# One layer of a streaming encoder on one core: the first two column pairs as 16 block products with four operands each, their kept units made in the second macro tile, and the output weights' sums kept in DRAM

## The chip, the core and the metric

The kernel runs on one core of a Trainium2 chip. The metric is the device time of one execution in microseconds (us), lower is better. Engines are named as the profile names them: PE is the matrix engine (TensorE), PEld its weight loads, DVE the vector engine (VectorE), ACT the scalar engine (ScalarE), POOL is GpSimd, and SP is the engine whose queue issues most DMAs here.

## The reference, cut to what matters

`x` is 4096 tokens by 1024 channels, `mem` 256 rows by 1024, all float32. One layer is computed:

```python
h = rms_norm(x, pre_norm)
proj = h @ w_in                    # 1024 x 5120: b, c, u of 1024 each, gate of 1536, mq of 512
p, gate, mq = proj[..., :3072], proj[..., 3072:4608], proj[..., 4608:]
z = c_gate * u; mix = b_gate * (conv_w[0]*z[t-2] + conv_w[1]*z[t-1] + conv_w[2]*z[t])
mem_o = memory_cross_attention(mq, mem, mem_norm, w_mem_kv)     # 4 heads of 128, 256 keys
y = (concat([mix, mem_o]) * silu(gate)) @ w_out                 # 1536 x 1024
x = x + rms_norm(y, post_norm)
```

## The kernel before, in words

**Products in three passes.** Each float32 operand is split into a high part (ACT copies it to `fp32r`, which rounds it) and a low part (DVE subtracts the high part). A block product of 512 x 128 weights with 512 x 512 tokens is 4 slices of the contraction by 3 matmuls (high x high, high x low, low x high), so 12 matmuls of 512 columns (`product`, lines L1438 to L1440).

**Seven products for eight.** The input projection is done by macro tiles of 1024 tokens (`MACROS` = 4) and by pairs of 2 x 128 output columns (`PAIRS` = 20). A pair over a macro tile is a 2 x 2 by 2 x 2 block product (halves of the contraction, of the columns and of the tokens), made with 7 products R1, R5, R6, R3, R7, R2, R4 instead of 8 (Strassen and Winograd's scheme). For this it needs sums of blocks on both sides. `x_in` holds the four normed blocks Y11, Y21 (tile 0) and Y12, Y22 (tile 1); `token_sum` (L1027) makes four sums of them in place, 128 x 2048 each; `operand_hi` (L737) and `operand_lo` (L1031) split the seven results into `hop_hi` and `hop_lo`. On the weights' side `weight_sum` (L1055) makes four sums for each pair out of the four raw chunks X11, X21, X22, X12, and `build_hi` (L692) and `split_lo` (L1060) put seven *units* for each pair into four `slots`.

**Units are made once.** Macro tile 0 builds its 140 units and SP writes each to `w_split` in DRAM (L502); macro tiles 1 to 3 load them back (`load_unit`, L485). `KINDS` gives what a pair is: two `m` (gate of the memory branch, through SiLU), then four groups of `c`, `u`, `b`, `g` (the convolution's inputs and its gate), then two `q`. Macro tiles 0 to 2 run them in this order; the last runs `q`, `q` first, since its steps also carry the memory attention.

**The start.** Tokens' squares are summed (ACT L664, DVE L1258 and L1260), a column sum on PE (`sum_first`, L1444) gives the mean squares, ACT the root, DVE the inverse and four diagonal blocks (`inverse`), PE spreads them over the partitions (`spread`, L1459), and DVE scales the rows (`norm`, L1002). The first two pairs run side by side (`FIRST_TWO`: product r of pair 0, then of pair 1, for r in turn), in separate banks. Pair 2 follows, its first product being product 14 counted from 0.

**The output projection** (stage `OUT`, 16 pairs of token tiles) uses the same scheme for the convolution's 1024 rows of `w_out`: the four blocks of `w_conv` are loaded into `x_in` in the last pair's time, `token_sum` makes the same four sums, and the seven splits follow. Each OUT pair has two more products, M0 and M1 (`add_memory`), for the memory branch; they use `WM_HI` and `WM_LO`, which lie in `x_in`'s place (as `x_r`, split at L963, L967 and L1414), so they can be made only when the sums are done with.

**What sets the order.** All queues are written by hand. Each engine runs its list in order, and a wait on a semaphore holds all that stands behind it. PE does product `step` of the macro tile, ACT and DVE follow it step by step with the evacuations (`evacuate`, `add`, `use`) and with the unit four steps ahead (`ahead`). In the last pair before a macro tile, ACT and DVE also make its operands. PE's `multiply` waits for its unit, for the operand (only in a macro tile's first pair), and for its bank to be read.

Of the kernel before, what the change touches and what calls it, by code (L numbers as in the profile page):

```python
# [5 lines left out]
P = 128  # L6
D = 1024
SEQ = 4096
T = 512
NT = SEQ // T  # L10
SUB = T // P
KT = D // P
# [22 lines left out]
UNITS0 = PAIRS * PRODUCTS  # L35
# [3 lines left out]
LAST_ROWS = list(range(18, PAIRS)) + list(range(18))  # L39
R1, R5, R6, R3, R7, R2, R4, M0, M1 = range(PRODUCTS + 2)  # L40
# [17 lines left out]
OUT_X_AT = {122: 0, 123: 1, 124: 3, 125: 2}  # L58
# [12 lines left out]

FIRST_TWO = [(p, r) for r in range(PRODUCTS) for p in range(2)]
ORDER = FIRST_TWO + [(p, r) for p in range(2, ALL_PAIRS) for r in range(PRODUCTS)]

# [13 lines left out]
BUILT = {u: n for n, u in enumerate(sorted([u for (p, r), u in UNIT_OF.items() if p < PAIRS or p >= ALL_PAIRS]  # L88
# [6 lines left out]


X11, X21, X22, X12, G0, G1 = range(6)
PLACE, TIMES, WAS = {}, {}, {}
for _p in list(range(PAIRS)) + list(range(ALL_PAIRS, ALL_PAIRS + OUT_PAIRS)):
    for _x in (X11, X21, X22, X12) if _p < PAIRS else (X11, X21, X22, X12, G0, G1):  # L100
        if _p < 2:
            _n = 3 * _p + _x if _x != X12 else CHUNKS + _p
        elif _p < PAIRS:
            _n = (0, 1, 3, 4, 2, 5)[(4 * _p + _x - 8) % CHUNKS]
# [10 lines left out]
def row_of(p):  # L115

    return p % PAIRS if p < (MACROS - 1) * PAIRS else LAST_ROWS[p % PAIRS]

# [10 lines left out]
def built_pair(p):  # L129

    return p if p < PAIRS else PAIRS + p - ALL_PAIRS


def trunk(nc, x, x_t, mem, in_gains, post_g, conv, w_in, w_kv, w_conv, w_mem, out):
# [6 lines left out]
    with ExitStack() as ctx:  # L141
# [14 lines left out]
        first_x12 = at("first_x12", R4 * HK * T * 4, [2, HALF])  # L156
# [40 lines left out]
        raw_kv = [raws[:, 0:2, :], raws[:, 2:4, :]]  # L197
        v_t = at("v_t", Q_AT + 4 * KB, [NM])
# [24 lines left out]
        bank_x = [psum[:, 2, :], psum[:, 6, :]]  # L223
        bank_b = [psum[:, 3, :], psum[:, 7, :]]
# [10 lines left out]
        w_split = nc.dram_tensor("w_split", [UNITS0, P, UNIT], f32, kind="Internal").ap()  # L235
        mem_kept = nc.dram_tensor("mem_kept", [NT * SUB, P, MH, P], f32, kind="Internal").ap()
        q_kept = nc.dram_tensor("q_kept", [MACROS, MH, 2, P, T], f32, kind="Internal").ap()
        m_kept = nc.dram_tensor("m_kept", [MACROS, MH, 2, P, T], f32, kind="Internal").ap()
        g_kept = nc.dram_tensor("g_kept", [NT * SUB, 2, P, HK, P], f32, kind="Internal").ap()
# [13 lines left out]

        w_sum = sem("w_sum")
        w_hi = sem("w_hi")
        w_lo = sem("w_lo")
        unit_done = sem("unit_done")

# [76 lines left out]

        WM_HI = [x_r[:, 0, 0:HK, :], x_r[:, 1, 0:HK, :]]
# [13 lines left out]
        def raw(p, x):  # L350
            n = PLACE[p, x]
            return raws[:, n, :] if n < CHUNKS else first_x12[:, n - CHUNKS, :]
# [4 lines left out]
        def raw_used(eng, p, x):  # L357

            if x in (X11, X21):
# [19 lines left out]
        def unit_source(p, r):  # L379
# [3 lines left out]
            return sums_in(p)[:, 0 if r in (R5, R3) else 1, :]  # L383

        def sums_in(p):

            return sqt if p == 1 else st_w
# [3 lines left out]
        SECOND = {R3: zb[:, 1, HALO:], R7: zb[:, 3, HALO:], R2: zb[:, 0, HALO:], R4: zb[:, 2, HALO:]}  # L391

        def temp(p, r):
            return SECOND[r] if p == 1 else TEMP[r]

        def silu_count(p, r):

            if p < 2:
                return 2 * ORDER_OF[r] - 1 + p
# [6 lines left out]
        def temp_free(eng, p, r):  # L406

            kind = kind_of(p)
            if kind in "qcy":
                eng.wait_ge({R3: c12_done, R7: c22_done, R2: c11_done}[r], p + 1)  # L410
# [5 lines left out]
        def sums_before(p, r):  # L416

            if p < 2:
                return 2 * min(r, 4) - 1 + p
# [29 lines left out]
        def normed_for(m, block):  # L449

            return 2 * KT * m + (("11", "12", "22", "21") if m == 0 else ("11", "21", "12", "22")).index(block) * HK + HK
# [6 lines left out]
        def _(sp):  # L458
            def load_raw(p, x):
# [3 lines left out]
                if p < PAIRS:  # L463
                    src = w_in[p, x]
# [11 lines left out]
            def load_x(n, m):  # L476
                tile, half = n % 2, n // 2
                src = x_t[2 * m + tile] if m < MACROS else w_conv[tile]
# [1197 lines left out]
```

## Time and profile before

| | us |
|---|---|
| median of 3 runs | 2240.54 (2238.6 to 2240.66) |
| the profiled execution, its time | 2240.83 |
| its span, first to last instruction | 2238.7 |
| PE busy | 2181.0 (97%) |
| DVE busy | 1213.8 (54%) |
| ACT busy | 734.6 (33%) |
| DMA | 462.64 MB, 207 GB/s on the mean |

PE is busy for 97% of the span, so what can be won beside fewer matmuls lies where PE isn't busy or is at its lower clock. A matmul's record is longer (0.39 us) than the distance between two starts (0.23 us), since they are pipelined: distances between starts tell the rate, and a distance of 0.43 us is the lower of PE's two clocks. The chain of waits that ended last is 88% PE.

### The profile page before, as it was taken

The page shows a single profiled execution, that of the slowest core. Times are in us where ns is not written, and L with a number is a line of the kernel's source. Part 1 is how long each engine was busy: PE and PEld are TensorE (multiplying, and loading weights), DVE is VectorE, ACT ScalarE, POOL GpSimd, SP SyncE. Part 2 cuts the span into 40 slices and gives each one's busy share as a digit, 9 for nine tenths or more (in the row PEclk, how much of TensorE's full clock was granted, in tenths as well). Part 3 has the DMA queues.
Part 4 walks back from the last instruction along what each step waited for, and adds up shares of the span by engine and source line. Part 5 has one row for each costly group of instructions (what it writes and reads, how often), then busy time and mean ns, then how long its engine had stood idle before and what let it go on. Part 6 is the DMA issues. An engine that isn't in the chain of part 4 may idle for free.

```text
span 2238.7 us, 26842 instructions
## 1 busy us (share of the span) xinstructions
PE 2181.0 (97%) x9950; PEld 1805.9 (81%) x9950; DVE 1213.8 (54%) x1917; ACT 734.6 (33%) x1328; POOL 100.8 (5%) x155
## 2 busy tenths in 40 slices
PE   5999999999999999999999999999999899999998
PEld 3788888788888888888888888888888688888886
DVE  7677787614443351444335337576755755555554
ACT  4433433411121131212113333535442533333332
POOL 0000000000000000000000000000010000000000
PEclk9999999999999999999999999999999999999999
DMA  4886676677566577756667666666667433434331
GB/s 170 309 307 255 256 272 245 253 262 256 187 209 212 194 245 268 252 186 211 207 213 259 226 215 197 215 201 215 198 203 295 129 130 109 132 132 132 127 119 65
DMA packets 140880, 462.64 MB, mean 207 GB/s; under 512 B 15664, under 2 KB 15696, under 8 KB 137808
## 3 DMA queue, kind: packets, MB, share of 16 engines
q1 hardware_dynamic: 119952, 385.40, 49.6%
q0 software_dynamic: 20800, 75.53, 10.4%
q8 instruction: 81, 1.33, 0.2%
q14 instruction: 47, 0.39, 0.1%
HBM read 328.75 MB, written 132.12 MB: 206 GB/s over the span
## 4 chain that ended last, share of the span: by engine, by line
PE 88%; DVE 6%; issue 2%; ACT 2%; DMA 1%; SPq 0%; DVEq 0%; ACTq 0%
PE banks L1438 29%; PE banks L1440 29%; PE banks L1439 29%; DVE hop_lo L1031 2%; PE banks L1553 1%; DVE x_in L1027 1%; DMA slots<-w_split 1%; ACT probs L811 0%; ACT hop_hi L737 0%; PE banks L1444 0%; DVE slots L1060 0%; PE banks L1459 0%; DMA raws<-in_w_kv 0%; DVE x_in L1002 0%; DVE rmax L1181 0%
## 5 line engine op out<-in xcount | busy, mean ns | idle before, releaser
L1438 PE MATMUL banks<-hop_hi,slots 128*128 128x512 f32 x2688 | 1055.9, 393 | 18.7 <-DVE slots L1060 6.7
L1439 PE MATMUL banks<-hop_lo,slots 128*128 128x512 f32 x2688 | 1048.8, 390 | 0.0
L1440 PE MATMUL banks<-hop_hi,slots 128*128 128x512 f32 x2688 | 1048.3, 390 | 0.0
L1438 PEld LDWEIGHTS banks<-hop_hi,slots 128*128 128x128 f32 x2688 | 506.1, 188 | 131.1 <-DVE slots L1060 14.4
L1440 PEld LDWEIGHTS banks<-hop_hi,slots 128*128 128x128 f32 x2688 | 506.0, 188 | 106.4
L1439 PEld LDWEIGHTS banks<-hop_lo,slots 128*128 128x128 f32 x2688 | 506.5, 188 | 103.7 <-issue 1.4
L1060 DVE TENSOR_TENSOR slots<-raws,slots 128x512 fp32r<-128x512 f32 x154 | 105.3, 690 | 130.9 <-ACT slots L692 130.4
L748 ACT ACTIVATE s<-banks 128x512 f32<-128x512 f32 x95 | 56.9, 599 | 343.8 <-PE banks L1440 343.0
L1112 DVE TENSOR_TENSOR u<-banks,u 128x512 f32<-128x512 f32 x55 | 38.0, 690 | 235.7 <-PE banks L1440 235.7
L692 ACT ACTIVATE slots<-raws 128x512 fp32r<-128x512 f32 x154 | 95.5, 626 | 150.4 <-PE banks L1440 126.3
L692 ACT ACTIVATE slots<-st_w 128x512 fp32r<-128x512 f32 x140 | 87.9, 628 | 158.8 <-PE banks L1440 121.2
L1060 DVE TENSOR_TENSOR slots<-st_w,slots 128x512 fp32r<-128x512 f32 x140 | 96.1, 686 | 29.4 <-ACT slots L692 29.0
L756 ACT ACTIVATE u<-banks 128x512 f32<-128x512 f32 x95 | 56.7, 597 | 156.2 <-PE banks L1440 156.2
L752 ACT ACTIVATE p<-banks 128x512 f32<-128x512 f32 x95 | 56.8, 597 | 149.6 <-PE banks L1440 149.6
L1438 PE MATMUL banks<-x_r,slots 128*128 128x512 f32 x256 | 100.3, 392 | 3.5 <-DVE x_r L1414 3.5
L1439 PE MATMUL banks<-x_r,slots 128*128 128x512 f32 x256 | 100.3, 392 | 0.0
L1440 PE MATMUL banks<-x_r,slots 128*128 128x512 f32 x256 | 100.1, 391 | 0.0
L1031 DVE TENSOR_TENSOR hop_lo<-x_in,hop_hi 128x2048 fp32r<-128x2048 f32 x35 | 79.6, 2286 | 27.1 <-ACT hop_hi L737 27.1
L737 ACT ACTIVATE hop_hi<-x_in 128x2048 fp32r<-128x2048 f32 x35 | 66.1, 1909 | 51.7 <-DVE x_in L1027 37.6
L620 POOL DMA_DIRECT2D g_kept<-mix x32 | 28.3, 888 | 985.5 <-DVE mix L1137 985.5
L811 ACT ACTIVATE probs<-banks,nmax 128x256 f32<-128x256 f32 x128 | 58.9, 473 | 29.9 <-DVE nmax L1183 29.9
L1196 DVE TENSOR_TENSOR pt_lo<-banks,pt_hi 128x512 fp32r<-128x512 f32 x64 | 41.2, 686 | 47.7 <-ACT pt_hi L819 47.2
(163 smaller groups left out, 1938.0 us busy)
## 6 DMA issues: line engine op xcount, KB each, us to landing
slots<-w_split SPq DMA_DIRECT2D x420, 512.0 KB, 3.4
w_split<-slots SPq DMA_DIRECT2D x140, 512.0 KB, 3.2
raws<-in_w_in SPq DMA_DIRECT2D x78, 256.0 KB, 3.9
x_in<-in_x_t SPq DMA_DIRECT2D x16, 1024.0 KB, 6.9
g_kept<-mix POOLq DMA_DIRECT2D x32, 512.0 KB, 6.6
raws<-g_kept SPq DMA_DIRECT2D x64, 256.0 KB, 3.9
x_zb<-in_x POOLq DMA_DIRECT2D x22, 512.0 KB, 4.2
out_x<-x_zb POOLq DMA_DIRECT2D x21, 512.0 KB, 4.1
```

Of the source, the lines that this page charges most:

```text
L692: nc.scalar.activation(slots[:, slot, 0, :], src, ACT.Copy).then_inc(w_hi, 1)
L737: nc.scalar.activation(hop_hi[:, r, :, :], Y_OF[r], ACT.Copy).then_inc(hop_hi_done, 1)
L748: nc.scalar.activation(temp(p, R2), a, ACT.Copy).then_inc(s1_done, 1)
L752: nc.scalar.activation(temp(p, R7), bank_x[p == 1], ACT.Copy).then_inc(p5_done, 1)
L756: nc.scalar.activation(temp(p, R3), a, ACT.Copy).then_inc(u2_done, 1)
L811: nc.scalar.activation(probs[:, n % 2, s, :], scores[:, s, :], ACT.Exp, scale=SCALE, bias=nmax[:, s:s + 1], accum_out=rsum[:, s:s + 1]).th ...
L1031: nc.vector.tensor_tensor(hop_lo[:, r, :, :], Y_OF[r], hop_hi[:, r, :, :].bitcast(f32), ALU.subtract).then_inc(hop_lo_done, 1)
L1060: nc.vector.tensor_tensor(slots[:, slot, 1, :], src, slots[:, slot, 0, :].bitcast(f32), ALU.subtract).then_inc(w_lo, 1)
L1196: nc.vector.tensor_tensor(pt_lo[:, a, :], probs_t[:, a, :], pt_hi[:, a, :].bitcast(f32), ALU.subtract).then_inc(pt_lo_done, 1)
L1438: nc.tensor.matmul(dst, a, c, start=first, stop=False, skip_group_check=True)
L1439: nc.tensor.matmul(dst, a, d, start=False, stop=False, skip_group_check=True)
L1440: return nc.tensor.matmul(dst, b, c, start=False, stop=last, skip_group_check=True)
```

## The change

1. **The first two pairs (both `m`) of macro tile 0** are no longer made with 7 products each. They are 16 plain block products (`multiply_first`), on four blocks of tokens and four raw weight chunks for each pair, without any sum. The eight chunks are split where `hop_hi` and `hop_lo` later have operands R7 and R4. The list runs tile 0 first (both halves of the contraction, both pairs), then tile 1; each of its four quarters needs one more block of tokens.
2. **The start is put in another order:** Y11 is split in two halves of its own, tile 0 is normed whole before tile 1's sums are used, and PE runs 50 matmuls of 128 x 128 float32 on constants (`warm`) ahead of the first column sums and 16 more ahead of the first product.
3. **Their 14 units** (rows 0 and 1 of `w_split`) are built in macro tile 1 instead, where the two `m` pairs stand behind the 16 convolution pairs (`SECOND_ROWS`, `LATE`): ACT and DVE build them four steps ahead, SP keeps them, and their raw chunks are loaded again. Everything that counts pairs from the first is counted from pair 2 (`seven_to`).
4. **The sums of `w_conv`'s blocks** are made in macro tile 2, a quarter at a time (4 x 4 sums of 128 x 512 on DVE, `out_sum`), and kept in DRAM (`sums_kept`). The seven operands of OUT are then loaded: four in the steps 122 to 125 as before, three more when the operand that held the place has been split. No `token_sum` is left in the OUT stage, and the splits follow each other one step apart.

Lines with only "..." stand for what is left out.

```diff
+DIRECT = 2
+UNITS0 = (PAIRS - DIRECT) * PRODUCTS
+SECOND_ROWS = list(range(DIRECT, 18)) + list(range(DIRECT)) + list(range(18, PAIRS))
+LATE = [PAIRS + SECOND_ROWS.index(n) for n in range(DIRECT)]
+LATE_RAW_AT = 96
+WARM = (50, 16)
-OUT_X_AT = {122: 0, 123: 1, 124: 3, 125: 2}
+OUT_X_AT = {122: R1, 123: R5, 124: R6, 125: R3}
+SUMS_MACRO = MACROS - 2
+SUMS_LOAD_AT = [1 + 10 * k for k in range(HK)]
+SUMS_AT = [a + 3 for a in SUMS_LOAD_AT]
+SUMS_KEEP_AT = [a + 8 for a in SUMS_LOAD_AT]
+FIRST_UNITS = [(p, x) for x in (X11, X21, X12, X22) for p in range(DIRECT)]
+FIRST = FIRST_UNITS + [(p, x) for half in ((X11, X21), (X12, X22)) for p in range(DIRECT) for x in half]
...
 SP: first loads
             load_x(0, 0)
             load_x(2, 0)
-            load_raw(0, X11)
+            for p in range(DIRECT):
+                load_raw(p, X11)
             load_x(1, 0)
+            for p in range(DIRECT):
+                load_raw(p, X21)
             load_x(3, 0)
...
 SP: macro tiles 1 to 3
+                        if p in LATE:
+                            keep_unit(p, r)
+                        else:
+                            load_unit(p, r)
+                        if m == SUMS_MACRO:
+                            out_sums_ahead(now)
...
+                        if now == (PAIRS - 1) * PRODUCTS + R5:
+                            sp.wait_ge(hop_lo_done, OUT * PRODUCTS + R1 + 1)
+                            load_out(R7)
+                        if now == (PAIRS - 1) * PRODUCTS + R6:
+                            sp.wait_ge(hop_lo_done, OUT * PRODUCTS + R5 + 1)
+                            load_out(R2)
...
+            sp.wait_ge(hop_lo_done, OUT * PRODUCTS + R6 + 1)
+            load_out(R4)
...
 ACT and DVE: units ahead
-                if m == 0 and n < UNITS0:
-                    build(*ORDER[n])
+                if m < 2 and n < STEPS and (m == 0 or PAIRS + n // PRODUCTS in LATE):
+                    build(m * PAIRS + n // PRODUCTS, n % PRODUCTS)
...
 ACT: in the last pair, then after it
-                    if i == PAIRS - 1 and r != R6 and (m + 1 < OUT or r != R4):
+                    if i == PAIRS - 1 and m + 1 < OUT and r != R6:
                         operand_hi(m + 1, {R1: R1, R5: R5, R3: R6, R7: R3, R2: R7, R4: R2}[r])
+                    if i == PAIRS - 1 and m + 1 == OUT and r != R4:
+                        operand_hi(OUT, r)
                 if n == 0:
-                    operand_hi(OUT, R2)
+                    operand_hi(OUT, R4)
...
 DVE: the start
             for n in range(1, HK + 1):
                 add_first(0, n)
+            first_units_lo(X11)
             inverse(0)
             add_first(1, 1)
             for k in range(HK):
                 norm(0, k)
+            for half in range(2):
+                two = slice(2 * half, 2 * half + 2)
+                dve.wait_ge(first_hop_hi, half + 1)
+                nc.vector.tensor_tensor(hop_lo[:, R1, two, :], Y11[:, two, :], ...)
+            add_first(1, 2)
+            first_units_lo(X21)
+            for n in range(3, HK + 1):
                 add_first(1, n)
+            for k in range(HK, KT):
+                norm(0, k)
+            first_units_lo(X12)
             inverse(1)
+            operand_lo(0, R2)
+            first_units_lo(X22)
+            for k in range(KT):
+                norm(1, k)
+            ... hop_lo[:, R6, :, :] from Y12, then operand_lo(0, R3)
             token_sum(0, 0)
+            build(DIRECT, R1)
+            operand_lo(0, R5)
...
 DVE: in the last pair before OUT
+                    if i == PAIRS - 1 and m + 1 == OUT and r != R1:
+                        operand_lo(OUT, r - 1)
...
 PE: the start
+            def multiply_first(n):
+                p, x = FIRST[n]
+                half = int(x in (X12, X22))
+                bank = first_output((n // 8 * 4) + (n % 4))[3]
+                if n < len(FIRST_UNITS):
+                    pe.wait_ge(first_unit_lo, n + 1)
+                if n and n % 4 == 0:
+                    pe.wait_ge(hop_lo_done, n // 4)
+                ... 12 matmuls
+            def warm(n):
+                for _ in range(n):
+                    nc.tensor.matmul(psum[:, 7, 0:P], ones[:], ones[:], start=True, stop=True)
             pe.wait_ge(consts_set, 5)
+            warm(WARM[0])
             sum_first(0)
             spread(0)
+            warm(WARM[1])
+            multiply_first(0)
+            multiply_first(1)
             sum_first(1)
+            multiply_first(2)
+            multiply_first(3)
             spread(1)
-            for p, r in FIRST_TWO:
-                multiply(p, r)
+            for n in range(4, len(FIRST)):
+                multiply_first(n)
```

## Rows read from the trace of the kernel before

**Rows 1.** Page: span, part 1 (busy time, share, instructions)
```profile
span 2238.7 us, 26842 instructions
PE 2181.0 (97%) x9950; PEld 1805.9 (81%) x9950; DVE 1213.8 (54%) x1917; ACT 734.6 (33%) x1328; POOL 100.8 (5%) x155
```
**Rows 2.** PE by stretch: stretch and length, busy (instructions), granted clock, DMA share, GB/s
```profile
100.00:385.00 285.00, 285.00 (x1263) 1.00 0.74 270
```
**Rows 3.** PE in order of time, start: start us, us, what [idle before <-releaser]
```profile
12.95 1.84 PE L1444 MATMUL banks<-ones,first_sq 128*128 128x1 f32 x8 [12.95 <-DVE first_sq L1260]
16.26 2.07 PE L1459 MATMUL banks<-acc,ones 128*128 128x512 f32 x2 [1.48 <-DVE acc L996]
29.97 0.76 PE L1438 MATMUL banks<-hop_hi,slots 128*128 128x512 f32 x1 [0.22 <-DVE hop_lo L1031]
...
41.53 0.79 PE L1438 MATMUL banks<-hop_hi,slots 128*128 128x512 f32 x1 [4.23 <-DVE slots L1060]
...
46.39 0.63 PE L1440 MATMUL banks<-hop_hi,slots 128*128 128x512 f32 x1
...
82.77 0.47 PE L1438 MATMUL banks<-hop_hi,slots 128*128 128x512 f32 x1 [2.38 <-ACT mix L782]
...
85.61 0.39 PE L1438 MATMUL banks<-hop_hi,slots 128*128 128x512 f32 x1
...
88.33 0.39 PE L1438 MATMUL banks<-hop_hi,slots 128*128 128x512 f32 x1
```
**Rows 4.** DVE in order of time, start
```profile
16.12 1.22 DVE L1258 TENSOR_TENSOR first_sq<-first_sq 128x1024 f32<-128x1024 f32 x1
18.37 2.72 DVE L1002 SCALAR_TENSOR_TENSOR x_in<-x_in,gains,banks 128x512 f32<-128x512 f32 x4 [1.03 <-PE banks L1459]
...
27.54 2.28 DVE L1031 TENSOR_TENSOR hop_lo<-x_in,hop_hi 128x2048 fp32r<-128x2048 f32 x1
```
**Rows 5.** ACT in order of time, start
```profile
3.48 0.20 ACT L862 ACTIVATE ysd<-eps 128x1 f32<-128x1 f32 x1 [1.45 <-POOL ident L599]
...
11.59 2.00 ACT L664 ACTIVATE first_sq<-x_in 128x1024 f32<-128x1024 f32 x2 [1.15 <-DMA x_in<-in_x_t]
...
16.88 1.14 ACT L692 ACTIVATE slots<-raws 128x512 fp32r<-128x512 f32 x2
21.13 1.91 ACT L737 ACTIVATE hop_hi<-x_in 128x2048 fp32r<-128x2048 f32 x1 [3.11 <-DVE x_in L1002]
```
**Rows 6.** PE in order of time, small matmuls at the full clock
```profile
186.26 0.95 PE L1444 MATMUL banks<-ones,acc 128*128 128x1 f32 x8
187.07 0.48 PE L1438 MATMUL banks<-hop_hi,slots 128*128 128x512 f32 x1
```
**Rows 7.** PE in order of time, around one head's transposes
```profile
1339.14 1.03 PE L1553 MATMUL banks<-ident,probs 128*128 128x128 f32 x8
1339.93 0.47 PE L1438 MATMUL banks<-hop_hi,slots 128*128 128x512 f32 x1
```
**Rows 8.** PE in order of time, where the OUT stage begins
```profile
1736.76 0.47 PE L1438 MATMUL banks<-hop_hi,slots 128*128 128x512 f32 x1 [1.75 <-DVE p L1112]
...
1746.88 0.47 PE L1438 MATMUL banks<-hop_hi,slots 128*128 128x512 f32 x1 [1.68 <-ACT s L748]
...
1760.87 0.47 PE L1438 MATMUL banks<-hop_hi,slots 128*128 128x512 f32 x1 [2.01 <-DVE mix L1112]
...
1767.30 0.64 PE L1438 MATMUL banks<-x_r,slots 128*128 128x512 f32 x1 [3.45 <-DVE x_r L1414]
```
**Rows 9.** DMA issues: what, times, KB each, median us to landing
```profile
slots<-w_split SPq DMA_DIRECT2D x420, 512.0 KB, 3.4
w_split<-slots SPq DMA_DIRECT2D x140, 512.0 KB, 3.2
x_in<-in_w_conv SPq DMA_DIRECT2D x4, 1024.0 KB, 7.3
```
**Rows 10.** PE in order of time, after the wait that ends macro tile 0
```profile
428.71 0.47 PE L1438 MATMUL banks<-hop_hi,slots 128*128 128x512 f32 x1 [2.04 <-DVE zb L1112]
...
430.80 0.63 PE L1438 MATMUL banks<-hop_hi,slots 128*128 128x512 f32 x1
```

More of the change, by code:

```diff
@@ L334, in trunk @@
         Y_OF = [Y11, Y12, Y12, Y22, Y11, Y21, Y21]
+        OUT_OF = [Y11, Y12, Y21, Y22, Y11, Y12, Y21]
+        OUT_LOAD = [(0, 1), (1, 1), (2, 1), (3, 1), (0, 2), (1, 2), (2, 2)]
         WM_HI = [x_r[:, 0, 0:HK, :], x_r[:, 1, 0:HK, :]]
@@ L491, in _ @@
             load_x(3, 0)
[L492 to L506 removed]
+            for x in (X12, X22):
+                for p in range(DIRECT):
+                    load_raw(p, x)
@@ L507, in _ @@
+            for x in (X11, X21, X22, X12):
+                load_raw(DIRECT, x)
+            for p, r in ORDER[:UNITS0]:
+                keep_unit(p, r)
+                if r == R1 and p < PAIRS - 1:
                     load_raw(p + 1, X11)
                     load_raw(p + 1, X21)
-                if r == R3 and 1 < p < PAIRS - 1:
+                if r == R3 and p < PAIRS - 1:
                     load_raw(p + 1, X22)
@@ L1279, in _ @@
                 norm(0, k)
-            for n in range(2, HK + 1):
+            for half in range(2):
+                two = slice(2 * half, 2 * half + 2)
+                dve.wait_ge(first_hop_hi, half + 1)
+                nc.vector.tensor_tensor(hop_lo[:, R1, two, :], Y11[:, two, :], hop_hi[:, R1, two, :].bitcast(f32),
+                                        ALU.subtract).then_inc(first_hop_lo, 1)
+            add_first(1, 2)
+            first_units_lo(X21)
+            for n in range(3, HK + 1):
@@ L1319, in _ @@
-            build(*ORDER[len(FIRST_TWO) + 3])
-            for p in range(2, ALL_PAIRS):
+            build(DIRECT, R6)
+            build(DIRECT, R3)
+            token_sum(0, 3)
+            operand_lo(0, R7)
+            operand_lo(0, R4)
+            for p in range(DIRECT, ALL_PAIRS):
                 m, i = divmod(p, PAIRS)
@@ L1347, in _ @@
                     ahead(m, step)
-                    if i == PAIRS - 1:
+                    if m == SUMS_MACRO:
+                        for k, first in enumerate(SUMS_AT):
+                            if first <= step < first + 4:
+                                out_sum(k, step - first)
+                    if i == PAIRS - 1 and m + 1 == OUT and r != R1:
+                        operand_lo(OUT, r - 1)
+                    if i == PAIRS - 1 and m + 1 < OUT:
                         if r in (R5, R6, R7, R2, R4):
@@ L1368, in _ @@
                             token_sum(m + 1, 0)
-                    elif step == 130:
-                        token_sum(OUT, 0)
                     if m + 1 == MACROS:
```

427 lines of the change are left out of this document (223 added, 204 removed).

## The prediction

> **What bounds the kernel now.** I read the page's busy times first: PE is busy 2181.0 of 2238.7 us [rows 1]. PE by stretch says where the rest is: from 100 to 385 us it is busy 285.00 of 285.00 at clock 1.00 [rows 2], as in most later stretches. There only fewer matmuls would help, and the change removes none. PE in order of time then shows two places with room: the start, up to pair 2's first product at 82.77 us [rows 3], and the begin of the OUT stage [rows 8]. One product of 12 matmuls takes 88.33 - 85.61 = 2.72 us at the full clock [rows 3], 0.227 a matmul.
>
> *Start.* PE's first product begins at 29.97, and 14 products are 38.1 us of work, so pair 2 could start at 68.1; it starts at 82.77. 14.7 us are lost to waits for DVE's and ACT's splits and sums (4.23 at 41.53, 2.38 at 82.77, and smaller ones) and to matmuls at the half clock. *OUT.* The idle times there are 1.75, 1.68, 2.01 and 3.45 [rows 8]; after the last, PE runs at the half clock (0.64 a record [rows 8], 0.43 from start to start, for 8 matmuls or 3.4 us: 0.2 lost on each, 1.7 in all). With some tenths at slots it is 11 us, and each idle time ends with a DVE or ACT instruction. DVE is the late one in both places: four `token_sum` and seven `hop_lo` splits at 2.28 each [rows 4].
>
> The profiled execution took 2240.83; the median of the runs is 0.3 less. I sum against 2240.83.
>
> **Part 1, the start.** Rates for back-to-back work: DVE 2.2 for 128x2048, 1.15 for 128x1024, 0.6 for 128x512, 0.66 a normed row (four in 2.72) [rows 4]; ACT 1.85, 1.0, 0.55 for the same sizes [rows 5].
>
> *The 50 matmuls of `warm`.* PE may start when the constants are there, 3.5 [rows 5]. A float32 matmul is two records (4 column sums are x8) [rows 3, 6]. Cold, 8 records took 1.84, 0.23 each [rows 3]; at the full clock they start 187.07 - 186.26 = 0.81 for 8, 0.10 each [rows 6]. Two records of 512 columns take 2.07 cold [rows 3], so at 128 columns the stream and the load are alike, about 0.107 at the full clock. 100 records are 10.7 us at the full clock and 3.5 + 10.7 = 14.2 is later than 12.95, where the column sums start now. The part run at the half clock counts double; the spell from 41.53 lasts to beyond 46.39 [rows 3], 5.3 us, that from 1767.30 3.4 us [rows 8], so I add 1.7 to 2.7. The warm matmuls end at about 16.2 (15.9 to 17.6), and the sums start 3.2 later than before, though they take 0.9 instead of 1.84.
>
> *From there:* column sums to 17.1; root, inverse and diagonals (1.48, as now [rows 3]) to 18.5; spread to 19.6; DVE adds once and norms four rows to 22.4; halves of the split on ACT and DVE (1.0 and 1.15) let the first product start at 23.7. The 16 warm matmuls (3.4) lie in that wait and cost nothing; without them PE would be idle for 4 us, and after 4.23 us idle it ran at the half clock [rows 3].
>
> *Then PE is the bound.* Two products end at 29.1; tile 1's column sums need DVE by then: after 24.8 it has 1.15 + 1.2 + 1.15 + 0.6, done at 28.9. Sums 0.8, two products, and spread 0.9 (the diagonals are ready at 33.9) give 36.3. Y21's split: norm to 31.6, ACT to 33.5, DVE (after 1.2 for X12 and 1.1 for the inverse) to 36.2, just in time. Y12's is ready at 44.8 and wanted at 47.2; Y22's at 47.0 and wanted at 58. The 16 products take 43.5 us, 5.4 more than 14. Pair 2 starts at 23.7 + 43.5 + 0.8 + 0.9 + 0.2 = 69.1, against 82.77: **13.7 less**. Its own operands (R5's at 54.5, R7's at 69.2, R4's at 73.5) come ahead of need (71.8, 80, 85). The loads change little: one more chunk and then two stand ahead of tile 1's halves, 0.6 us each, and its first half now lands at 11.59 [rows 5]; at 12.3 it is still ahead of the sums.
>
> **Part 2, the late units.** 14 units less in the start, 14 more in macro tile 1: 22 sums and splits of 0.6 on DVE and 14 of 0.55 on ACT, in 14 steps of 2.72. In macro tile 0 the same work stands beside every pair and PE is never idle [rows 2]. SP's `keep_unit` waits for the split, about 1.3 us after a slot is free, and behind it stands the next step's keep or load, wanted 2.7 later. Kept units land in 3.2, loads in 3.4 [rows 9], with 8.2 to spare for a load. Cost 0; if the cover is gone, a load that is late costs its excess (0 to 1).
>
> **Part 3, the sums in macro tile 2.** 16 DVE operations of 0.6 in steps of which DVE uses half; 4 x 1 MB loaded and kept in 34 steps. SP waits for the keep two steps (5.4 us) after its issue. A 1 MB load took 7.3 [rows 9], so SP may stand 2 us with a unit's load 8.2 - 3.4 = 4.8 ahead. Cost 0, bound 1.
>
> **Part 4, the OUT stage.** Four `token_sum`s (8.8 us) leave DVE. I laid its list again over the times of before. PE's R4 starts at 1736.76 after 1.75 idle [rows 8], so R2 ended at 1735.0, R7 at 1732.3, R3 at 1729.6. DVE adds R3 (1730.3), sums and splits R1's unit, for which ACT must first load the SiLU table behind R6's high part (1732.4), and splits operand R6 (1734.6). From here each step is add, `use`, sum, unit's split, operand's split, 4 x 0.6 + 2.2: R7's result is added at 1735.2, so R4 starts at 1735.35; R2's at 1739.8; the last pair's `use` of R2 ends at 1744.4. For that ACT's evacuation of OUT's R1 waits (0.6), and for this PE's R6, since R4, R1 and R5 end at 1743.5: R6 starts at 1745.2 (was 1746.88). From there the splits R2 (1747.8), R4 (1751.2) and the memory weights' (1755.2, 1758.6) come before PE wants them, and M0 starts at 1759.05, where PE has run without a wait, against 1767.30: 8.2. With no idle time over 1.8 the half clock after it goes too, 1.7: **9.9 less**. What is late next is DVE still, 0.4 us ahead of M0. The three late loads are issued at 1726.2, 1728.9 and 1734.6 and wanted at 1736.9, 1741 and 1745.8; with 7.3 each [rows 9] the last has 4 to spare, and nothing else waits on SP but the memory weights, wanted at 1749 and 1752.
>
> *A rule weighed.* After 1.75 and 1.68 us idle PE kept its full clock [rows 8]; after 2.04, at 428.71, it ran at the half clock from the fourth matmul on, some 8 of them, 1.6 us [rows 10]. My sum takes nothing for the remaining 1.7 us wait. The Trainium skill ("TensorE: Matmul & The Clock Gate", "Why this matters for your kernels") says no idle gap above about 3 us for the clock to hold; by that rule too the sum takes nothing, but the row at 428.71 disagrees with it, and by that row it would be 1.6 more.
>
> **Sum:** 2240.8 - 13.7 - 9.9 = 2217.2; against the median 2217.
>
> **The rivals.**
> 1. *The warm matmuls hide.* If they are as quick as the transposes (8 of 128 columns in 1339.93 - 1339.14 = 0.79, one record each [rows 7]), 50 are 5 us plus some 2 for the cold part, over by 10.5, ahead of 12.95. Then the whole start comes 3.2 earlier: 2214. For it: same sizes; against: a float32 product is two records. The Trainium skill ("TensorE: Matmul & The Clock Gate", "Back-to-back issue gap") has 56 ns for a matmul of 128 columns at the full clock, with which this outcome would come too; the column sums' 0.10 a record [rows 6] speak against it.
> 2. *The clock doesn't hold in the start*: idle gaps of 1.4 (root, inverse) after 16.2, or a rise that comes late, leave the first product or the warm list at 1.2 GHz. Half a spell of 5.4 us like that at 41.53 to two of them: +2.7 to +5.4, 2221.
> 3. *The OUT stage gives back half*: `hop_lo` splits one step apart leave DVE no room (2.2 + 4 x 0.6 = 4.6 us in a step of 2.72), or a late load holds ACT, so M0 starts at about 1764: 2222.
> 4. *Slower*: the late units choke. A slot of macro tile 1 can be filled again only when its keep has landed. That is hidden while a keep takes under 10.9 - 1.3 = 9.6 us; each us above is paid in 14 steps. To be slower than before, all 23.6 must go: 11.3 a keep, where the median is 3.2 [rows 9]. Price at 11.5: 14 x 1.9 = 27, 2244; at 12 it is slower, 2251.
>
> **How the numbers follow.** Forecast 2217: 0.56. Rival 1 (2214): 0.18. Rival 2 (2221): 0.12. Rival 3 (2222): 0.10. Rival 4: 0.04. The range of 2211 to 2225 takes all but rival 4 and the tails of 2 and 3. A measurement of this kernel can tell 0.2% (4.5 us) from no change. Faster by more than that 0.95, within it 0.02 (rivals 3 and 2 together with late loads), slower 0.03 (rival 4).
>
> **What would show each step.** In PE's order of time: the first column sums at about 16.2, the first product at 23.7 with records of 0.4, sixteen products without a wait over 0.3, pair 2 at 69. DVE's four splits of 128x2048 in the OUT stage 4.6 apart without L1027's operation between them, the first matmul on `x_r` 8 us earlier against the last pair. In macro tile 1's late steps no idle time of PE. The prediction is wrong if PE waits for a unit of the late pairs, if the column sums start at 13 (rival 1), or if records of 0.63 fill the first product (rival 2).

## The result, and the profile after

The changed kernel takes 2221.48 us in the median of 4 runs (2220.31 to 2223.02), beside 2240.6 (2238.6 to 2241.83) for the kernel before on the same chip: a ratio of 0.9915, with an interval of 0.9903 to 0.9927. That is 0.85% faster, 19 us. The forecast was 2217 with a range of 2211 to 2225: the sign and the range hold, and the time is 4.5 us above the number. The profiled execution took 2222.47, 18.4 less than that of before. Its page has, with the span and busy times to be set beside [rows 1]:

```profile
span 2220.6 us, 27170 instructions
PE 2191.1 (99%) x10106; PEld 1821.0 (82%) x10106; DVE 1218.6 (55%) x1933; ACT 739.1 (33%) x1332; POOL 100.8 (5%) x155
```

PE is busy for 10 us longer (among other things by the 66 warm matmuls, and by 16 products for 14) in a span that is 18 us shorter. PE in order of time shows where the span was shortened. These are lines of the changed kernel at the start, at the end of macro tile 0, in macro tile 2 and in the OUT stage (start, duration, what, the idle time before it and what ended it). They answer to [rows 3], [rows 10] and [rows 8]; L1541 is what L1438 was, a slice's first matmul, L1547 the column sums (L1444), L1562 the spread (L1459), and L1714 the warm matmuls.

```profile
3.50 14.18 PE L1714 MATMUL banks<-ones 128*128 128x128 f32 x100 [3.50 <-POOL ident L711]
17.51 0.95 PE L1547 MATMUL banks<-ones,first_sq 128*128 128x1 f32 x8
19.94 1.12 PE L1562 MATMUL banks<-acc,ones 128*128 128x512 f32 x2 [1.48 <-DVE acc L1108]
20.90 3.73 PE L1714 MATMUL banks<-ones 128*128 128x128 f32 x32
25.11 0.47 PE L1541 MATMUL banks<-hop_hi 128*128 128x512 f32 x1 [0.47 <-DVE hop_lo L1392]
...
70.61 0.39 PE L1541 MATMUL banks<-hop_hi,slots 128*128 128x512 f32 x1
...
416.43 0.47 PE L1541 MATMUL banks<-hop_hi,slots 128*128 128x512 f32 x1 [2.04 <-DVE zb L1226]
...
850.29 0.50 PE L1541 MATMUL banks<-hop_hi,slots 128*128 128x512 f32 x1 [1.57 <-DMA slots<-w_split]
...
880.12 0.50 PE L1541 MATMUL banks<-hop_hi,slots 128*128 128x512 f32 x1 [2.32 <-DMA slots<-w_split]
...
1726.69 0.47 PE L1541 MATMUL banks<-hop_hi,slots 128*128 128x512 f32 x1 [0.42 <-DVE p L1226]
1736.81 0.47 PE L1541 MATMUL banks<-hop_hi,slots 128*128 128x512 f32 x1 [1.71 <-ACT s L860]
1750.83 0.46 PE L1541 MATMUL banks<-x_r,slots 128*128 128x512 f32 x1
```

The same points of PE's list in the two profiled executions:

| PE starts | before | after | less by | this part |
|---|---|---|---|---|
| first column sums | 12.95 | 17.51 | -4.6 | |
| first product | 29.97 | 25.11 | 4.9 | |
| pair 2 | 82.77 | 70.61 | 12.2 | start: -12.2 |
| prefetched sums, macro tile 0 | 186.26 | 173.98 | 12.3 | |
| the same, macro tile 1 | 574.59 | 561.34 | 13.25 | clock: -1.0 |
| a later spread (L1562, before L1459), macro tile 1 | 683.40 | 670.14 | 13.3 | |
| prefetched sums, macro tile 2 | 959.74 | 951.04 | 8.7 | given back: +4.6 |
| transposes | 1339.14 | 1330.63 | 8.5 | |
| first matmul on `x_r` | 1767.30 | 1750.83 | 16.5 | OUT: -8.0 |
| PE's last | 2228.45 | 2210.38 | 18.1 | clock: -1.6 |

Two things stand out against the prediction. The start gives 12.2 instead of 13.7, and between 670 and 951 us 4.6 are given back. That stretch holds the late units (ahead of 810) and the sums of `w_conv` (behind it). PE's busy time, clock, DMA share and rate there, in the changed kernel:

```profile
674.00:810.00 136.00, 136.00 (x601) 1.00 0.69 242
810.00:946.00 136.00, 131.76 (x579) 1.00 0.86 306
```

The late units cost nothing. The loss lies in macro tile 2, where the kernel before has, for the same work:

```profile
822.00:958.00 136.00, 135.66 (x599) 1.00 0.75 252
```

Both waits of that stretch are for a weight unit from DRAM. What SP issued ahead of the first of them (start, time in issue, line):

```profile
832.80 0.43 SPq L563 DMA_DIRECT2D sums_kept<-raws  x1
835.16 3.04 SPq L571 DMA_DIRECT2D slots<-w_split  x2
840.45 1.21 SPq L558 DMA_DIRECT2D raws<-in_w_conv  x2
841.71 0.60 SPq L571 DMA_DIRECT2D slots<-w_split  x1
```

A unit's load goes out every 2.72 us when SP is free. The third of those that begin at 835.16 was due at about 840.6. SP stood instead at the next quarter's wait for the keep that it had issued at 832.80, which landed 7.6 us later, issued two raw loads (1.2 us), and came to the unit's load at 841.71, 1.1 late. That load landed 8.5 us later, in a stretch with this landing time of the units' loads (size, median us), where a load had 3.4 over the whole kernel before [rows 9]:

```profile
slots<-w_split SPq DMA_DIRECT2D x44, 512.0 KB, 5.6
```

A unit may take 8.16, three steps, from its slot's release to PE's need. 1.1 + 8.5 - 8.16 is 1.4; PE waited 1.57. At the second wait it is the same again: the keep at 861.87, SP at the raw loads at 869.62, the unit's load at 870.88, 1.2 late, and 2.32 of idle time. The two waits are 3.9 us idle. From start to start they cost 1.7 and 2.5 us, and the next start behind each follows after 0.34 instead of 0.23; that is 4.4 of the 4.6.

### The profile page after: what moved, and what is told of

It is laid out like the page before. It is cut to its first block, busy times and chain, and to the rows that moved or that the text cites. A ratio compares the mean times of both kernels' runs of the same rounds, so it can differ in the third digit from the quotient of the medians.

```text
span 2220.6 us, 27170 instructions
## 1 busy us (share of the span) xinstructions
PE 2191.1 (99%) x10106; PEld 1821.0 (82%) x10106; DVE 1218.6 (55%) x1933; ACT 739.1 (33%) x1332; POOL 100.8 (5%) x155
## 4 chain that ended last, share of the span: by engine, by line
PE 89%; DVE 5%; DMA 3%; issue 2%; ACT 1%; SPq 0%; POOL 0%; DVEq 0%; ACTq 0%; POOLq 0%
PE banks L1541 29%; PE banks L1543 29%; PE banks L1542 29%; DVE hop_lo L1146 2%; DMA slots<-w_split 1%; PE banks L1658 1%; DMA sums_kept<-raws 1%; PE banks L1714 1%; DVE x_in L1132 1%; DMA q_kept<-zb 0%; ACT probs L917 0%; PE banks L1562 0%; ACT hop_hi L849 0%; DVE rmax L1295 0%; PE banks L1547 0%
## 5 line engine op out<-in xcount | busy, mean ns | idle before, releaser
L1541 PE MATMUL banks<-hop_hi,slots 128*128 128x512 f32 x2632 | 1030.8, 392 | 10.3 <-DMA slots<-w_split 5.1
L1542 PE MATMUL banks<-hop_lo,slots 128*128 128x512 f32 x2632 | 1024.7, 389 | 0.0
L1543 PE MATMUL banks<-hop_hi,slots 128*128 128x512 f32 x2632 | 1024.6, 389 | 0.0
L1541 PEld LDWEIGHTS banks<-hop_hi,slots 128*128 128x128 f32 x2632 | 494.3, 188 | 117.2 <-issue 10.1
L1543 PEld LDWEIGHTS banks<-hop_hi,slots 128*128 128x128 f32 x2632 | 494.1, 188 | 103.3
L1542 PEld LDWEIGHTS banks<-hop_lo,slots 128*128 128x128 f32 x2632 | 494.4, 188 | 101.2 <-issue 1.4
L1541 PE MATMUL banks<-x_r,slots 128*128 128x512 f32 x256 | 99.7, 389 | 0.0
```

The costliest lines, as they stand in the source:

```text
L1541: nc.tensor.matmul(dst, a, c, start=first, stop=False, skip_group_check=True)
L1542: nc.tensor.matmul(dst, a, d, start=False, stop=False, skip_group_check=True)
L1543: return nc.tensor.matmul(dst, b, c, start=False, stop=last, skip_group_check=True)
```

## The experiments

The parts are numbered here as in the prediction: part 1 is the start, part 2 the late units, part 3 the sums in macro tile 2, part 4 the OUT stage (parts 3 and 4 are together the fourth item of the change).

**The theory.** (a) The sums of `w_conv` cost about 4 us, by the queue that stands at the keep and by the busy DMA together; (b) the start's remainder is the warm matmuls' length; (c) the OUT stage and the late units are as predicted. **Rivals:** the sums cost by their traffic alone, wherever they are put and whatever SP does; the rest of the loss lies in the OUT stage; or the warm matmuls are too few to hold the clock. The medians below are of 4 or 5 runs, beside runs of the kernel before on the same chip (medians 2239.76, 2240.05 and 2241.73 on three chips).

### r1_changed, the changed kernel again

> The changed kernel itself, as the reference for the three beside it. Expected 2221.5 us (its four runs gave 2220.3 to 2223.0). In the start the first column sums at 17.5, the first product at 25.1, pair 2 at 70.6; in macro tile 2 two waits of PE for a unit's load, 1.6 and 2.3 us.

2222.12 (2220.3 to 2223.78), ratio 0.9922 [0.9908, 0.9935]. Its profiled execution, 2220.38, shows how much moves from run to run: the warm matmuls took 12.82 us instead of 14.01, PE's two waits for units were 1.5 in sum instead of 3.9, and the half clock came behind the 2.04 us wait at the end of macro tile 0, where the other execution kept the full one.

Four traces have the keep two steps ahead of SP's wait, in the busy stretch: the changed kernel's, this one, r2_warm28's and r4_no_warm's. Each has three places where SP comes to such a wait with a unit's load behind it. The load is due 5.44 us behind the first unit's load that follows the keep. Read off SP's and PE's order of time:

| | first place: load late by, PE's wait | second | third |
|---|---|---|---|
| changed kernel | 1.1, 1.57 | 1.2, 2.32 | 0, none |
| r1_changed | 1.4, 1.32 | 0, none | 0, 0.18 |
| r2_warm28 | 2.8, 2.45 | 0.1, none | 1.3, 1.61 |
| r4_no_warm | 0.8, 1.33 | 1.4, 2.63 | 1.4, 0.89 |

Where the load goes out late, PE waits (eight of eight); where it is at most 0.1 late, PE waits 0.18 at most (four of four).

### r3_sums_apart and r9_apart_again: the sums in a quieter stretch

```diff
-SUMS_LOAD_AT = [1 + 10 * k for k in range(HK)]
+SUMS_LOAD_AT = [44, 54, 74, 84]
```

> The sums of w_conv's blocks at steps 44, 54, 74 and 84 of macro tile 2 instead of 1, 11, 21 and 31, clear of the loads of x (steps 20 to 41), of m_kept's writes (14, 21) and of g_kept's. Theory A (PE's waits of 1.6 and 2.3 us there are units' loads that share the DMA engines with those 1 MB transfers): both waits go, 3.9 less: 2217.6. Rival B (the waits come from the sums' own traffic and the wait on the queue for the keep, wherever it is): the waits move along, 2221.5, with SP held 2 us at each keep. Rival C (DVE's 16 operations are what costs): no wait for a load, but PE waits for DVE, 2221 or more.

> The kernel with the sums at steps 44, 54, 74, 84 again, as the reference for the two beside it, which differ from it in the matmuls on constants: 2218.3 (2217.4 to 2219.0 in its first runs).

2218.33 (2217.38 to 2218.95) and 2217.78 (2217.38 to 2218.5): 3.8 and 4.3 less than r1_changed, and with a smaller scatter. No wait for a unit is left in these two traces. In r3_sums_apart PE needs 276.34 us (670.09 to 946.43) from macro tile 1's later spread to macro tile 2's prefetched sums, exactly the 276.34 of the kernel before (683.40 to 959.74); that stretch has the late units and the first quarter's loads, and from 925 to 1080, where all four quarters lie, PE is busy for 155.00 of 155.00 us. So late units and sums together cost nothing there. SP waits less for its keep. Its queue in r3_sums_apart, around one of the keeps:

```profile
950.62 0.43 SPq L563 DMA_DIRECT2D sums_kept<-raws  x1
952.97 3.04 SPq L571 DMA_DIRECT2D slots<-w_split  x2
956.77 1.21 SPq L558 DMA_DIRECT2D raws<-in_w_conv  x2
958.41 0.33 SPq L571 DMA_DIRECT2D slots<-w_split  x1
```

The DMA share of its stretch is 0.76 to 0.78, not 0.86, the keep lands in 6.15 instead of 7.6, and so the unit's load behind the raw loads still goes out on time (958.41 is 5.44 behind 952.97). It does at every keep of this run. A unit's load takes at most 7.6:

```profile
DMA to landing us min/median/max: 3.1/4.4/7.6
```

So this run took away two things at once, the late issue and the busy stretch; it does not show what a late issue would cost on a quieter DMA. It does not make the stretch safe either: r10_no_warm_apart (below) has its sums at the same steps, at a share of 0.75, every unit's load on time, and one of them, issued at 1040.87, landed 9.2 us later:

```profile
1050.12 0.50 PE L1541 MATMUL banks<-hop_hi,slots 128*128 128x512 f32 x1 [1.12 <-DMA slots<-w_split]
```

With the sums at these steps r7_warm28_apart has a wait of 0.3 and r8_bridge one of 0.2.

### r6_keep_earlier: the same stretch, the queue not held

```diff
-SUMS_KEEP_AT = [a + 8 for a in SUMS_LOAD_AT]
+SUMS_KEEP_AT = [a + 7 for a in SUMS_LOAD_AT]
```

The transfers, their sizes and their stretch stay; only the keep has three steps instead of two until SP waits for it.

> Each quarter of the sums is kept one step earlier (7 steps after its load instead of 8), so SP's wait for it at the next quarter's load is 2.7 us shorter: 0 instead of 2.2. Theory A1 (PE's waits there come from SP being held: the unit's load behind the wait goes out 1.1 us late): the waits shrink by 1.1 each, 2219.3. Theory A2 (they come from sharing the DMA engines with 1 MB transfers alone): 2221.5, with waits of 1 to 2.5 us as before.

2217.78 (2216.9 to 2218.75), ratio 0.9899 [0.9886, 0.9913]: 4.3 less than r1_changed, as much as moving the sums away, and more than the 2.2 that theory A1 had added up. SP's queue around the same keep:

```profile
829.74 0.56 SPq L563 DMA_DIRECT2D sums_kept<-raws  x1
832.09 5.76 SPq L571 DMA_DIRECT2D slots<-w_split  x3
837.89 1.21 SPq L558 DMA_DIRECT2D raws<-in_w_conv  x2
840.25 0.33 SPq L571 DMA_DIRECT2D slots<-w_split  x1
```

The raw loads go out 8.15 behind the keep, and the unit's load is on time at 840.25. PE's stretch from 810 to 946 is busy for 135.62 of 136 us, at a DMA share of 0.87 and 312 GB/s, more than the changed kernel moved. The loads' median is nearly the same, but no load passes the 8.16 that it has. The changed kernel's line for 44 loads (805 to 930 us), then that of r6_keep_earlier for 45 (min, median, max):

```profile
DMA to landing us min/median/max: 3.1/5.6/9.9
```
```profile
DMA to landing us min/median/max: 3.2/5.5/8.1
```

So the traffic alone isn't the cause, which was the rival. With the same traffic and the loads on time PE doesn't wait; r11_warm28_keep, with the same keep, has no such wait either. That the busy DMA has its share in it is argued from the numbers: a load 1.1 late costs nothing unless it takes over 7.1 to land, and in r3_sums_apart the median was 4.4. No run has a late load on a quieter DMA. Nor is it settled why the longest load shrank from 9.9 to 8.1 with the issue on time: behind a late issue, two raw loads and up to two units' loads are issued within 3 us of each other and may share the DMA engines. The wait of r10_no_warm_apart, whose unit's load was on time but only 1.5 us behind the first of two raw loads, fits that; no run separates it.

### r5_undo_out: the OUT stage and the sums as before

The fourth item of the change is taken back whole, which is parts 3 and 4 of the prediction; the start and the late units stay. Of its diff:

```diff
-OUT_X_AT = {122: R1, 123: R5, 124: R6, 125: R3}
+OUT_X_AT = {122: 0, 123: 1, 124: 3, 125: 2}
...
-                        if m == SUMS_MACRO:
-                            out_sums_ahead(now)
...
+                    elif step == 130:
+                        token_sum(OUT, 0)
```

> Part 4 undone, all else as in the changed kernel: no sums of w_conv's blocks in macro tile 2 and none in DRAM; the four token sums, the loads and the order of the splits in the OUT stage are those of the kernel before. Theory A (the OUT stage's 9.6 us come from the four sums that left DVE, and part 4 pays 3.7 of it back in macro tile 2): 2221.5 + 9.6 - 3.7 = 2227.4, with PE's four waits of 1.7, 1.7, 2.0 and 3.4 us back ahead of the first matmul on x_r and none of a unit's load in macro tile 2. Rival B (the OUT stage was won by something else in the change, as an earlier or quieter arrival): the four waits don't come back, 2217.8.

2224.70 (2224.11 to 2227.24), ratio 0.9933 [0.9921, 0.9946]. Theory A's mechanism holds, the four waits are back; its time of 2227.4 was 2.7 too high. Parts 1 and 2 alone are worth 15.4 us. In this run's trace pair 2 starts 13.4 earlier than in the kernel before (69.38 for 82.77); where the other 2 us of the medians lie no trace shows. As for the rest, parts 3 and 4 together bring 2.6 with the stall (against r1_changed) and 6.9 without it (against r6_keep_earlier). PE in order of time in r5_undo_out, to be set beside [rows 8]:

```profile
1723.67 0.47 PE L1536 MATMUL banks<-hop_hi,slots 128*128 128x512 f32 x1 [1.75 <-DVE p L1222]
1733.79 0.47 PE L1536 MATMUL banks<-hop_hi,slots 128*128 128x512 f32 x1 [1.69 <-ACT s L849]
...
1747.78 0.47 PE L1536 MATMUL banks<-hop_hi,slots 128*128 128x512 f32 x1 [2.00 <-DVE mix L1222]
1753.99 0.47 PE L1536 MATMUL banks<-x_r,slots 128*128 128x512 f32 x1 [3.24 <-DVE x_r L1512]
```

In the profiled executions PE ends at 2215.15 here and at 2205.47 in r6_keep_earlier, 9.7 apart, while the medians are 6.9 apart. From the transposes to the first matmul on `x_r` it is 427.73 here (1326.26 to 1753.99) and 420.23 there (1325.69 to 1745.92): the waits are worth 7.5. Behind 1753.99 r5_undo_out runs at the half clock, which is 1.6 more, and 0.6 lie ahead of the OUT stage. Its profiled execution was the longest of its five (2224.11 to 2227.24), so the 1.6 are probably not in all of them; the other four left no trace that could say.

### r4_no_warm and r10_no_warm_apart: no warm matmuls at all

```diff
-WARM = (50, 16)
+WARM = (0, 0)
```

r10_no_warm_apart has `SUMS_LOAD_AT = [44, 54, 74, 84]` beside it, so that the stall of macro tile 2 doesn't cover the difference.

> No matmuls on constants at all. Theory A: the column sums start at 12.6 at the half clock (1.84 us), the spread takes 2.1, so the first product comes at about 22, 3.1 earlier than with 50 and 16, but runs 3.4 to 5.9 us at the half clock and loses 1.7 to 2.9: between 2220.1 and 2221.3, so within 1.5 us of the changed kernel. Rival B (a cold start costs more, since later waits let the clock fall again, as the half-clock spell after 41.53 in the kernel before): two spells, 2222 to 2224.

> No matmuls on constants, sums at steps 44, 54, 74, 84, so that macro tile 2's waits don't blur the comparison. Theory (what 66 matmuls win in clock, 50 of them lose by delaying the column sums, since both starts reached tile 0's next column sums at 173.9 us): 2218.3, within 1 us of the one beside it. Rival (they do win something): 2220 to 2221.

2221.42 (2220.49 to 2225.91) beside r1_changed's 2222.12, and 2218.16 (2217.64 to 2218.8) beside r9_apart_again's 2217.78 (2217.38 to 2218.5): no difference in either pair. PE's start in r10_no_warm_apart:

```profile
12.83 1.84 PE L1547 MATMUL banks<-ones,first_sq 128*128 128x1 f32 x8 [12.83 <-DVE first_sq L1374]
...
22.26 0.77 PE L1541 MATMUL banks<-hop_hi 128*128 128x512 f32 x1 [4.04 <-DVE hop_lo L1392]
...
29.52 0.95 PE L1547 MATMUL banks<-ones,first_sq 128*128 128x1 f32 x8
```

and in r9_apart_again with the 66:

```profile
24.83 0.47 PE L1541 MATMUL banks<-hop_hi 128*128 128x512 f32 x1 [0.47 <-DVE hop_lo L1392]
```

Without them the first product starts 2.6 us earlier and runs at the half clock (0.77), and tile 1's column sums, two products later, come 0.8 earlier (29.52 for 30.36). At macro tile 0's prefetched sums it is still 0.8 ahead (172.80 and 173.59 us), a lead that this execution gives back at its 1.12 us wait for a unit. But the warm start's own length varies as much: over the six traces with 66 warm matmuls these sums come at 172.74 to 173.98, over the two without any at 172.80 and 173.86. So the two starts are level within what these traces scatter: what the warm matmuls win in clock they cost in delay. r4_no_warm's profiled execution is one of its two slowest (2225.59); it has three waits for units, 4.9 us in sum, and its scatter is theirs more than the start's.

### r2_warm28, r7_warm28_apart and r11_warm28_keep: 28 of them

```diff
-WARM = (50, 16)
+WARM = (28, 16)
```

r7_warm28_apart adds the sums' place of r3_sums_apart, r11_warm28_keep the keep of r6_keep_earlier.

> 28 instead of 50 matmuls on constants ahead of the first column sums. Theory A (the 50 matmuls are longer than the wait they fill: 3.50 to 17.51, while DVE's sums are ready at 12.6): 56 records end at about 3.5 + 5.9 + 29 x 0.112 = 12.65, so all of the start comes 4.8 us earlier: 2216.7, with the first product at 20.3 and at the full clock. Rival B (the clock needs the long run of matmuls: with 28 it falls back in the 1.5 us for root and diagonals or before the first product): 8 to 14 matmuls at the half clock give back 1.7 to 2.9: 2219. Rival C (something else in the start is as late, a load or DVE, so that it gains nothing): 2221.5.

> 28 matmuls on constants and the sums at steps 44, 54, 74, 84. If the two costs are independent: the start 3.3 to 3.6 earlier (the first product at 21.6 instead of 25.1) on top of the 3.8 of the sums: 2214.5. If the earlier start is eaten later by a wait that does not move (a load, POOL's writes), 2218.

> 28 and 16 matmuls on constants, and each quarter of the sums kept one step earlier. Theory: the start wins 2.5 to 3.5 on 2217.8: 2215, and no wait for a unit's load of more than 0.3 us in macro tile 2, though the three quarters lie beside the loads of x. If the result of the earlier keep hung on where those loads fell, waits come back: 2218.

2220.62 (2219.11 to 2223.96), 2216.03 (2213.66 to 2216.54) and 2215.82 (2214.99 to 2217.02). The first is within the scatter of the stalls (its trace has two waits for a unit, 2.45 and 1.61 us, and the half clock behind the first); in the other two 28 are worth 2 us: r9_apart_again has 2217.78, r6_keep_earlier 2217.78. All three gain less than was summed for them (2216.7, 2214.5, 2215). PE's start in r2_warm28:

```profile
3.51 8.85 PE L1714 MATMUL banks<-ones 128*128 128x128 f32 x56 [3.51 <-POOL ident L711]
12.72 1.05 PE L1547 MATMUL banks<-ones,first_sq 128*128 128x1 f32 x8 [0.36 <-DVE first_sq L1374]
15.45 2.08 PE L1562 MATMUL banks<-acc,ones 128*128 128x512 f32 x2 [1.68 <-DVE acc L1108]
17.32 4.38 PE L1714 MATMUL banks<-ones 128*128 128x128 f32 x32
21.57 0.47 PE L1541 MATMUL banks<-hop_hi 128*128 128x512 f32 x1
```

The column sums wait for DVE again, not for PE, and the first product starts at 21.57, 3.5 earlier than with 50. Part of it is lost: the spread ran at the half clock (2.08 for 1.12) and the 16 that follow took 4.38 for 3.73, so that they and not DVE release the first product. In r7_warm28_apart and r11_warm28_keep the same 16 took 5.14 and 5.31, and the first product starts at 22.31 and 22.47.

### r8_bridge: six matmuls in that gap

The six go between column sums and spread of tile 0, on r7_warm28_apart:

```diff
             sum_first(0)
+            warm(6)
             spread(0)
```

> As the one beside it, with 6 more matmuls on constants between the first column sums and the spread, in the 1.5 us for root and diagonals. In the run with 28 alone the spread took 2.1 and the 16 matmuls 4.4 us, since the clock had fallen; theory: with the 1.5 us filled it doesn't fall, the spread takes 1.0 and the first product comes at 20.4, 1.1 earlier: 2213.3. Rival: the clock falls anyhow or the 6 matmuls are late and hold the spread: 2214.5 to 2215.

2215.70 (2213.55 to 2216.74) beside 2216.03: no gain. In r8_bridge PE's start reads:

```profile
13.71 2.50 PE L1714 MATMUL banks<-ones 128*128 128x128 f32 x12
16.01 1.81 PE L1562 MATMUL banks<-acc,ones 128*128 128x512 f32 x2
...
21.86 0.47 PE L1541 MATMUL banks<-hop_hi 128*128 128x512 f32 x1 [0.47 <-DVE hop_lo L1392]
```

The twelve records ran until 16.01 and held the spread 0.5 us beyond the 15.54 at which it starts in r7_warm28_apart; the 16 took 3.73 again, the full clock's time, and the first product starts 0.45 earlier than there (21.86 for 22.31), a lead that this execution lost at the end of macro tile 0, where it fell to the half clock and the other did not. The granted clock (the column behind the count) in r7_warm28_apart, then in r8_bridge:

```profile
12.80:14.00 1.20, 1.20 (x8) 0.80 1.00 411
14.00:16.00 2.00, 0.49 (x2) 0.50 0.97 390
```
```profile
12.80:14.00 1.20, 1.20 (x10) 1.00 1.06 437
14.00:16.00 2.00, 2.00 (x12) 0.54 0.96 384
```

The clock fell in r8_bridge while PE was busy, and in r7_warm28_apart while it still made the column sums, which end at 14.03, ahead of the 1.5 us gap. So in these two the gap for root and diagonals, which the six were to fill, is not what lowered it (in r2_warm28 the clock did fall inside that gap), and the rival of this run, that the clock falls anyhow, holds.

**Which kernel is best.** r7_warm28_apart, r8_bridge and r11_warm28_keep, at 2215.7 to 2216.0 with ratios of 0.9884 to 0.9889, are level with each other; they beat the kernel before by 24 to 26 us and the changed one by 5.5 to 6.

## Why the prediction was right, and where it was 4.5 us off

Sign and range hold, and so do the mechanisms of the start, the late units and the OUT stage; the one cost that was put at nothing without enough reason is part 3's. Of the 18.4 us in the profiled executions 12.2 come from the start and 9.6 from the OUT stage. By its own steps, summed against the profiled 2222.47: 2217.2, + 1.5 in the start, - 1.0 for a clock that didn't fall behind macro tile 0, + 4.6 in macro tile 2, + 0.3 in the OUT stage, is 2222.6.

**Part 1, a term mis-sized by 1.3 us.** Warm matmuls until 16.2 were predicted, within 15.9 to 17.6; they ended at 17.51, and in r1_changed at 16.32. The rate was taken too low: 32 records took 3.73, 0.117 each, where 0.107 had been read off shorter operations. 100 records are 11.7 then and not 10.7. What is left of the 14.0 is 2.3, and 1.1 in r1_changed, where 1.7 to 2.7 had been taken for the half clock. The chain behind them is right link for link: column sums 0.95, 1.48 for root and inverse, first product 7.6 us behind the sums (predicted 7.5), no wait in the sixteen products, and pair 2 45.5 behind the first product, predicted 45.4. What the step left out is whether they pay. It took the 16 as free and the 50 as the price of the clock, and never summed the start without them; r10_no_warm_apart did, and it comes to the same time, with pair 2 at 69.44 where the kernel before had 82.77. So the start's 12 us come from the plain block products and the new order, not from the warm matmuls; no run separates those two.

**Rival 1** (the warm matmuls hide, 2214) fell: 100 records last until behind 12.95, as the two records of a float32 product say. Its idea has something in it all the same: with 28 they do nearly hide, and that is worth 2 us. The page "TensorE: Matmul & The Clock Gate" of the Trainium skill ("Back-to-back issue gap") gives 56 ns for a matmul of 128 columns by itself and about 81 ns in a stream of weight loads and matmuls. Here a float32 one took two records of 117 ns, more than either.

**Rival 2** (the clock in the start, 2221) gave nearly the time, by another way. In the changed kernel the first product runs at full clock (0.47), so the mechanism didn't act. It does with 28 warm matmuls, where the first product came at 21.57 to 22.47 instead of the 20.3 summed for r2_warm28.

**Part 2, right.** Cost 0 was predicted, and 136.00 of 136.00 us were busy. **Rival 4** put the choke at the late units; the cost came some 130 us later, at the sums.

**Part 3, the step that failed.** Predicted 0 with 1 as a bound; 4.6 in the profiled execution and about 4 in the medians (r3_sums_apart, r9_apart_again, r6_keep_earlier). The wait was seen: "SP may stand 2 us with a unit's load 8.2 - 3.4 = 4.8 ahead". The hold was sized well (7.6 - 5.4 is 2.2; with the raw loads the unit's load came 1.1 late). What was wrong is the 3.4, the median landing over the whole kernel, taken unchanged under 8 MB more: the two loads that PE waited for took 8.5 and 9.2, and the median there was 5.6. In this stretch of the kernel before the DMA share is 0.75 already, and its loads land in 4.3 in the median and 6.8 at most:

```profile
DMA to landing us min/median/max: 3.2/4.3/6.8
```

From 6.8 the room is 1.4 and not 4.8, before 8 MB are added. With the stand of 2.2 that is already 0.8 over, so that stretch's largest landing would have given a cost in place of none, though not one of 4.6.

**Part 4, right.** Waits of 0.35 and 1.7 us were predicted, 0.42 and 1.71 are there, and the one at `x_r` is gone. DVE's splits are 4.72 apart, where the sum had 4.6:

```profile
1723.65 2.29 DVE L1146 TENSOR_TENSOR hop_lo<-x_in,hop_hi 128x2048 fp32r<-128x2048 f32 x1
1728.37 2.29 DVE L1146 TENSOR_TENSOR hop_lo<-x_in,hop_hi 128x2048 fp32r<-128x2048 f32 x1
```

The gain up to the first matmul on `x_r` is 8.0, predicted 8.2, and 1.6 more follow at full clock, predicted 1.7. **Rival 3** fell with it. A gain in the OUT stage was paid for in macro tile 2, though: parts 3 and 4 are one edit, and without r6_keep_earlier's one step it keeps 2.6 of its 6.9 us.

**The rule weighed.** The remaining wait of 1.71 cost no clock, as the sum had it. Of the 2.04 us wait at the end of macro tile 0 the kernels don't agree with each other: the half clock followed in the kernel before [rows 10] and in r1_changed, and not in the execution at the top, with the same idle time to the hundredth. The half clock came there in five of the thirteen traces (the kernel before, r1_changed, r4_no_warm, r5_undo_out, r8_bridge). Nor is its price the 1.6 us that I took from the row: from the prefetched sums of macro tile 0 to those of macro tile 1 PE needs 388.33 us with it and 387.36 without (the kernel before and the changed one), 1.0 more. Part of the loss is given back by a wait of 0.34 for ACT some 14 us on, which only the faster execution has.

## What to carry to other kernels

Before work is put into an in-order DMA queue, take the largest landing of the loads behind it in that very stretch, not the kernel's median, and add the time that the queue may stand at a wait; if the sum passes the prefetch distance, expect the compute engine to wait for the excess (here 1.1 + 8.5 against 8.16 gave 1.57), and the added traffic makes the landings longer still. Where a queue has to wait for its own write, issuing the write one step earlier can be worth as much as moving the whole work away (4 us here, with the same transfers). Warm-up matmuls are no free gain: sum the start without them as well, and let them end before the first real operation can start.

## What the runs showed of the hardware that wasn't expected

- The same idle time of 2.04 us on PE at the same place was followed by a granted clock of 1.2 GHz in five traces and of 2.4 GHz in eight. In macro tile 2 idle times of 2.45 us (r2_warm28) and 2.63 (r4_no_warm) were followed by the lower clock, 2.32 (the changed kernel) was not.
- After 28 warm matmuls the clock fell between 13.5 and 15.3 us in all four traces, in r8_bridge (0.54 granted from 14 to 16 us) with PE busy at the time; after 50 it kept its full value through an idle time of 1.48 us.
- The same 100 records of warm matmuls took 12.81 to 14.01 us between executions. That more of them ran at the lower clock in the longer ones is likely, but the trace has no granted clock below 1.00 there that would show it.
- With a DMA share of 0.86 a 512 KB load from DRAM took 5.6 us in the median and 9.9 at most, with 0.76 to 0.78 it took 4.4 and 7.6, with 0.75 in r10_no_warm_apart 4.1 and 9.2, and over the whole kernel before 3.4 in the median.
